# Sparse attention's rotated logits as products over 32 rows in four strips of rows, heads grouped by parity

## What is computed

```python
def block(args):                       # 128 queries at a time
    qf, qi, wi, qc = args
    s_idx = jax.nn.relu(jnp.einsum('bqhd,bkd->bqhk', qi, k_idx))
    score = jnp.einsum('bqh,bqhk->bqk', wi, s_idx)
    score = jnp.where(adm[None], score, -jnp.inf)
    _, sel = lax.top_k(score, topk)    # 128 keys a query
    ...
    logits = jnp.einsum('bqhc,bqkc->bqhk', qf, kv_sel) * scale
    p = jax.nn.softmax(logits, axis=-1)
    return jnp.einsum('bqhk,bqkc->bqhc', p, kv_sel[..., ROPE_DIM:])
```

## Time and profile before

| | |
|---|---|
| median of 3 runs | 2895.94 us (2895.63 to 2901.64) |
| span of the profiled execution | 2884.6 us |
| PE busy in the span | 2535.0 us (88%) |
| DVE busy in the span | 1498.1 us (52%) |
| chain that ended last: PE / DVE / DMA | 60% / 18% / 13% |
| sparse stage, in the span | about 376 to 628 us |
| L952 and L953, records | 80 and 80 |
| L1138 on POOL | 32 operations, median 602 ns |

### The profile page before, as it was taken

The page is one execution under the profiler, slowest core; times in us unless marked ns, Lnnn a source line. Parts: engine busy times, 40 slices in busy tenths (PEclk is TensorE's granted clock), DMA queues, the critical chain, the costliest instruction groups (busy, mean ns, idle before and its releaser), DMA issues.

```text
span 2884.6 us, 35666 instructions
## 1 busy us (share of the span) xinstructions
PE 2535.0 (88%) x14451; PEld 1940.8 (67%) x14451; DVE 1498.1 (52%) x3249; ACT 841.2 (29%) x1455; POOL 793.1 (27%) x755
## 2 busy tenths in 40 slices
PE   5997898889687878769989976789999999999998
PEld 5684544357444444448766566689999989998887
DVE  3125655645200000014543999869987878764443
ACT  2114322233100000014432237734333333333332
POOL 0002310000100000010000139745565656633342
PEclk8997999999799999988999988799999999999999
DMA  8224400014599999963114003799999999989995
GB/s 319 116 88 179 175 30 29 30 61 175 214 422 420 423 421 423 421 266 111 63 54 182 30 26 112 242 375 351 362 388 378 376 354 375 387 334 357 346 357 198
DMA packets 192104, 719.00 MB, mean 249 GB/s; under 512 B 32248, under 2 KB 69152, under 8 KB 162752
## 3 DMA queue, kind: packets, MB, share of 16 engines
q1 hardware_dynamic: 128960, 490.15, 43.7%
q0 software_dynamic: 62976, 226.52, 20.5%
HBM read 659.06 MB, written 57.16 MB: 248 GB/s over the span
## 4 chain that ended last, share of the span: by engine, by line
PE 60%; DVE 18%; DMA 13%; ACT 3%; issue 3%; POOL 2%; SPq 1%; POOLq 0%; DVEq 0%; ACTq 0%
PE psum L3286 9%; PE psum L3273 9%; DMA arena<-w 8%; PE psum L1592 5%; PE psum L426 4%; PE psum L2648 4%; PE psum L2112 4%; PE psum L3235 3%; PE psum L929 3%; DVE arena L3422 3%; DVE rounded L3371 3%; PE psum L1599 2%; DMA arena<-v_rows,arena 2%; PE psum L1201 2%; PE psum L1216 1%
## 5 line engine op out<-in xcount | busy, mean ns | idle before, releaser
L3286 PEld LDWEIGHTS psum<-rounded,rounded 128*128 128x128 f32 x3072 | 453.1, 189 | 34.6 <-issue 30.0
L3286 PE MATMUL psum<-rounded,rounded 128*128 128x320 f32 x3072 | 463.9, 311 | 10.6 <-ACT arena L3338 8.0
L3273 PEld LDWEIGHTS psum<-rounded,rounded 128*128 128x128 f32 x2880 | 426.0, 189 | 28.4 <-issue 13.9
L3273 PE MATMUL psum<-rounded,rounded 128*128 128x320 f32 x2880 | 434.8, 311 | 7.9 <-DVE rounded L3371 4.5
L3222 POOL DMA_INDIRECT arena<-u_rows,arena x192 | 279.6, 1456 | 254.9 <-DVE arena L3422 150.3
L1592 PE MATMUL psum<-arena 128*64 128x256 f32 x2048 | 261.7, 420 | 82.2 <-issue 61.6
L3312 ACT ACTIVATE rounded<-arena 128x1024 fp32r<-128x1024 f32 x248 | 256.9, 1050 | 263.0 <-PE psum L3286 187.1
L3371 DVE TENSOR_TENSOR rounded<-arena,rounded 128x1024 fp32r<-128x1024 f32 x248 | 303.1, 1222 | 18.4 <-ACT rounded L3312 18.4
L1592 PEld LDWEIGHTS psum<-arena 128*64 128x64 f32 x2048 | 183.8, 152 | 172.2 <-issue 123.7
L3222 POOL DMA_INDIRECT arena<-v_rows,arena x192 | 217.4, 1132 | 237.2 <-PE psum L3235 158.2
L1704 DVE COPY arena<-psum 128x256 f32<-128x256 f32 x32 | 13.6, 425 | 445.5 <-PE psum L1645 445.5
(11 more groups left out here) (453 smaller groups left out, 3337.4 us busy)
## 6 DMA issues: line engine op xcount, KB each, us to landing
arena<-w SPq DMA_DIRECT2D x96, 2048.0 KB, 25.8
arena<-v SPq DMA_DIRECT2D x64, 1024.0 KB
arena<-uT SPq DMA_DIRECT2D x60, 1024.0 KB
arena<-wada SPq DMA_DIRECT2D x12, 2048.0 KB
arena<-wp SPq DMA_DIRECT2D x10, 2048.0 KB
arena<-gd SPq DMA_DIRECT2D x60, 320.0 KB
gd<-arena SPq DMA_DIRECT2D x8, 2048.0 KB, 16.3
xb<-arena SPq DMA_DIRECT2D x1, 12032.0 KB, 42.1
```

The source lines that it names most:

```text
L3273: ins = pe.matmul(PS[:, b, 0:DT], w[:, x, k, :], hv[:, y, :], k == 0 and i == 0, k == 7 and i == 2)
L3286: ins = pe.matmul(PS[:, b, 0:DT], w[:, y, x, :], gg[:, z, :], x == 0 and i == 0, x == 7 and i == 2)
```

## The change

The rotated products are done over 32 rows instead of 128. A strip of 32 rows of the array holds the 16 rows of two heads, 2h and 2h + 1, so `QM` now leaves one head of the two: it is masked by the parity of the head, and a group g is the heads of one parity (0, 2, 4, 6 and 1, 3, 5, 7) instead of the first or last four. The four products of a group lie in four different strips of rows (`tile_position`). In blocks 0 to 2 each head of the group gets a bank of its own, 0 to 3. In block 3 two heads are done at a time, since each needs two banks.

The order on TensorE is changed with it: first the latent products of all heads of a batch (four heads, two in block 3), then all their rotated products, where before each head had its own two products in a row. `QM` is made once a block, for both groups, in two buffers; GpSimd first adds three pairs of mask columns into `PARITY`. `OLAT` and `QLAT` are indexed by head 2h + g.

```diff
+    def logit_bank(n, h):
+        return h if n < 3 else 2 * (h % 2)
...
-            pe.wait_ge(*D.po["qm", n, g])
-            for h in range(4):
-                b = 2 * (h % 2)
-                claim(*range(b, b + np_))
+            pe.wait_ge(*D.po["qm", n])
+            for hs in ((0, 1, 2, 3),) if np_ == 1 else ((0, 1), (2, 3)):
+                for h in hs:
+                    b = logit_bank(n, h)
+                    claim(*range(b, b + np_))
+                    for i in range(np_):
+                        pe.matmul(PS[:, b + i, 0:w], QLAT[:, 2 * h + g, 128 * n:128 * n + 128], CKT[:, i * w:i * w + w],
+                                  True, False)
                 for i in range(np_):
-                    pe.matmul(PS[:, b + i, 0:w], QLAT[:, 4 * g + h, 128 * n:128 * n + 128], CKT[:, i * w:i * w + w], True, False)
-                    ins = pe.matmul(PS[:, b + i, 0:w], QM[:, h, :], KR[:, i * w:i * w + w], False, True)
-                ins.then_inc(*D.pe("logits", n, g, h))
+                    for h in hs:
+                        r0 = 32 * h
+                        ins = pe.matmul(PS[:, logit_bank(n, h) + i, 0:w], QM[n % 2][r0:r0 + 32, g, :],
+                                        KR[r0:r0 + 32, i * w:i * w + w], False, True, tile_position=(r0, 0))
+                        if i == np_ - 1:
+                            ins.then_inc(*D.pe("logits", n, g, h))
...
     def sparse_po(po):
-        before = None
+        m8 = CST[:, C_M8:C_M8 + 8]
+        po.tensor_tensor(PARITY, m8[:, 0:2], m8[:, 2:4], ALU.add).then_inc(*D.po("parity", 0))
+        for x in (1, 2):
+            po.wait_ge(*D.po["parity", x - 1])
+            po.tensor_tensor(PARITY, PARITY, m8[:, 2 + 2 * x:4 + 2 * x], ALU.add).then_inc(*D.po("parity", x))
+        po.wait_ge(*D.po["parity", 2])
         for n in range(4):
+            if n > 1:
+                po.wait_ge(*D.pe["logits", n - 2, 1, 3])
             for g in range(2):
-                if before is not None:
-                    po.wait_ge(*before)
-                for h in range(4):
-                    ins = po.tensor_scalar(QM[:, h, :], RB[:, 128 * n:128 * n + 128],
-                                           CST[:, C_M8 + 4 * g + h:C_M8 + 4 * g + h + 1], None, ALU.mult)
-                ins.then_inc(*D.po("qm", n, g))
-                before = D.pe["logits", n, g, 3]
+                ins = po.tensor_scalar(QM[n % 2][:, g, :], RB[:, 128 * n:128 * n + 128], PARITY[:, g:g + 1], None, ALU.mult)
+            ins.then_inc(*D.po("qm", n))
```

More of the change, by code:

```diff
@@ L883, in build @@
     RS = [at(o_va + TK * i, TK) for i in range(2)]
-    QM = at3(o_va + 2 * TK, 4, 128)
+    QM = [at3(o_va + 2 * TK + 256 * i, 2, 128) for i in range(2)]
     PB = at3(OW, 4, TK)
@@ L892, in build @@
     SM = at(o + 12, 4)
-    assert o + 16 <= ARENA
+    PARITY = at(o + 16, 2)
+    assert o + 18 <= ARENA
     GAB = at3(2 * RING, 16, T)
@@ L946, in logits @@
             nk, np_, w = keys_of(n)
-            pe.wait_ge(*D.po["qm", n, g])
-            for h in range(4):
-                b = 2 * (h % 2)
-                claim(*range(b, b + np_))
-                for i in range(np_):
-                    pe.matmul(PS[:, b + i, 0:w], QLAT[:, 4 * g + h, 128 * n:128 * n + 128], CKT[:, i * w:i * w + w], True, False)
-                    ins = pe.matmul(PS[:, b + i, 0:w], QM[:, h, :], KR[:, i * w:i * w + w], False, True)
-                ins.then_inc(*D.pe("logits", n, g, h))
-                for x in range(b, b + np_):
-                    bank[x] = D.dv["logits", n, g, h]
+            pe.wait_ge(*D.po["qm", n])
[6 more added lines that the diff above has]
+                                  True, False)
+                for i in range(np_):
+                    for h in hs:
[4 more added lines that the diff above has]
+                            ins.then_inc(*D.pe("logits", n, g, h))
+                for h in hs:
+                    b = logit_bank(n, h)
+                    for x in range(b, b + np_):
+                        bank[x] = D.dv["logits", n, g, h]
         def latent(n, g):
@@ L1037, in sparse_ac @@
                 ac.wait_ge(*D.pe["latent", n, g])
-                ac.activation(OLAT[:, 4 * g:4 * g + 4, 128 * n:128 * n + 128], PS[:, 6, :].rearrange("p (a b) -> p a b", a=4),
-                              ACT.Copy).then_inc(*D.ac("latent", n, g))
+                ac.activation(OLAT[:, :, 128 * n:128 * n + 128].rearrange("p (h g) t -> p g h t", g=2)[:, g],
+                              PS[:, 6, :].rearrange("p (a b) -> p a b", a=4), ACT.Copy).then_inc(*D.ac("latent", n, g))
                 before = D.pe["latent", n, g]
```

## The result

| | before | changed | |
|---|---|---|---|
| median of 20 runs | 2898.86 us | 2910.42 us | ratio 1.0044, 95% interval 1.0028 to 1.0061 |
| lowest and highest | 2883.52, 2906.57 | 2896.09, 2926.13 | |
| span of the profiled execution | 2884.6 us | 2912.6 us | +28.0 |
| sparse stage in it | 251.1 us | 262.7 us | +11.6 |
| end of the stage to end of span | 2256.0 us | 2272.3 us | +16.3 |

The change makes the kernel 12.8 us slower by the ratio (8 to 18), where 8.6 was forecast (2904.5, range 2899 to 2910).

A forecast was written before the change was run, and what follows sets the result against it. VectorE's start and duration were taken to bound blocks 1 and 2, TensorE block 3. Terms 0.9 + 0.8 + 1.6 + 1.3 + 1.6 + 1.6 + 0.8 = 8.6 us gave span 2893.2, plus 11.3: 2904.5 us, range 2899 to 2910.

The forecast's parts named there:

- Which engine bounds: Sparse stage: VectorE's start and duration count in blocks 1 and 2, (0, 0) alike; TensorE bounds block 3.
- The first add at 5c + 0.4: Blocks 0 to 2, c one full product's time: VectorE's first add 1.6, 2.7, 3.8 us after the group's first product.
- Four strips at once: Rotated products on TensorE: four strips run together, so a set costs c, the time of one full product.
- The two changes of shape: TensorE, between full rows and strips: 0.2 us each way.
- VectorE's pace: Add and maximum per head: about 0.57 us at 144 columns, 0.91 at 272, 1.13 at 400.
- the groups with a slow clock: Groups (0, 1) and (1, 1), logits made at half clock: +0.8 and +1.3 us.
- two more stretches of 3.4 us: High end of the forecast's spread: two more stretches at half clock, within a loss of 13.3 us.
- signs of being wrong: Rotated product starting before the last latent ends, first add by 5c/2 or sooner, or slow clock without a pause ahead.
- The base: Time the loss was added to: profiled span 2884.6 us and 11.3 us around it.
- TensorE as the bound after all: Rival, blocks 0 to 3: TensorE's shorter part counts, -7.8 us, 2888.1 us; chance 0.06.
- Strips that don't overlap: Rival: strips overlap in pairs or not at all, each set c or 3c more, 2907 to 2916 us; chance 0.10.
- The clock that gives it back: Rival: slow stretches fall into longer pauses, loss 4.8 us, 2900.7 us, no change; chance 0.22.

The follow-up runs named there:

- e4: Kernel before plus unneeded TensorE products in its pauses, three per group of block 1, six per group of block 2: stage 242.8 us, ratio 0.9959 to before.
- e3: Changed kernel plus unneeded TensorE products in its pauses, four per group of block 1, six per group of block 2: stage 257.1 us, ratio 0.9996 to before.
- e2: Changed kernel with the rotated products in strips first, then each head's latent products: stage 251.4 us, ratio 1.0008 to before.
- g1: Changed kernel plus one unneeded TensorE product per group of blocks 1 and 2, in the pauses: stage 266.4 us, ratio 1.0049 to before, one run of each.
- f3: Changed kernel with four gates moved into TensorE's pauses of blocks 1 and 2: stage 234.0 us, ratio 0.9944 to before.
- e1: Kernel before with only the changed order and banks, products over full rows, no strips: stage 263.1 us, ratio 1.0026 to before.
- g2: Changed kernel plus unneeded TensorE products in pauses, two per group of block 1, three per group of block 2: stage 259.0 us, ratio 1.0060, one run of each.
- f2: Changed kernel with strips first, then each head's latent products, and four gates moved into TensorE's pauses of blocks 1 and 2: stage 221.0 us, ratio 0.9917 to before.

## Why the prediction was right and wrong

**Which engine bounds** was right, and with it the sign: the kernel got slower, by more than the noise. In (1, 0) the chain runs through VectorE, and TensorE's wait for the copy grew from 2.9 us to 4.1:

```profile
PE psum L986 <- DVE arena L1137: 4.1, 1, 4.1
...
PE psum L979 <- DVE arena L1130: 0.9, 1, 0.9
```

I had named 5.4. The second line is where most of the rest went: the gate now ends before the last division (L1130), so TensorE waits there too, 6.9 us in the stage, which I had not seen coming. It costs nothing by itself, since VectorE is the later one.

**The first add at 5c + 0.4** was right to 0.01 us at 272 columns, and to 0.05 in the others: 1.62 us at 144 columns (1.6), 3.75 at 400 (3.8) and 3.07 in block 3 (3.1). Four strips at once was right too. The two changes of shape, put at 0.2 us each, took 0.3 together at 144 and 272 columns and 0.4 at 400. The chain of block 3, answering:

```profile
591.16 1.78 PE psum L958 x8
592.95 1.14 PE psum L963 x8
594.09 0.70 DVE arena L1121
...
596.18 1.16 PE psum L958 x4
597.33 1.09 PE psum L963 x8
598.42 7.08 PE psum L934 x16
```

The chain goes over to VectorE between the two batches, as I had it: TensorE waits for the banks. The gate starts 7.35 us after the group's first product (598.35 - 591.00; 7.12 before, 7.5 forecast).

**VectorE's pace** was misread. The adds of the kernel before stand 0.91 us apart, and that is 2c = 0.92, the pace of TensorE's two products a head, not VectorE's own. With the logits ready VectorE needs 0.82 us a head, and 1.09 at 400 columns. So having all heads at once did win something: (1, 0) cost 1.3 us and not 1.6, (2, 0) 1.4. The adds of block 2 in the kernel before, 1.34 us apart, are at 2c as well.

**The term that failed is "the groups with a slow clock"**: +0.8 for (0, 1) and +1.3 for (1, 1), and nothing for TensorE's work behind VectorE's copy. Block 0 held (+1.9 for 1.7). Block 1 was forecast at 1.6 + 1.3 = 2.9 and measured 7.8. What follows the copy in (1, 1), before and in the changed kernel:

```profile
493.90 2.18 PE L972 MATMUL psum<-arena 128*128 128x512 f32 x4 [2.70 <-DVE arena L1123]
496.01 8.83 PE L929 MATMUL psum<-arena 128*128 128x512 f32 x16
...
500.94 4.07 PE L986 MATMUL psum<-arena 128*128 128x512 f32 x4 [4.08 <-DVE arena L1137]
504.94 9.60 PE L934 MATMUL psum<-arena 128*128 128x512 f32 x16
```

Up to this point block 1 lost 1.3 us in (1, 0) and 2.1 in (1, 1), 3.4 us, near the 2.9 of the forecast. The other 4.4 us lie behind the copy, where I had put nothing: the second piece of `latent` went from 2.2 to 4.0 us in (1, 0) and from 2.1 to 4.0 in (1, 1), and the gate from 8.8 to 9.5, all by half clock. I let the stretch of 3.4 us stay as it was and only asked whether it would fall into the pause. It became 10.2 us, twice, and in (1, 0) to (1, 1) took in the products L986, all the logits and the head of the gate. TensorE had taken up work again at 477.18 and did not pause, yet the clock stayed at half until 486.00. I had a bound of two more stretches of 3.4 us in the range; the four stretches of blocks 1 and 2 grew by 20.4 us together, six such stretches and not two, 13.6 us of it in block 1. In block 2 it went the other way (1.4 for 3.2): its longer stretches lay in the pauses, and the kernel before had paid for half clock there as well, 5.0 us by e4. The Trainium skill says that pauses of TensorE between bursts throw the clock back (TensorE: Matmul & The Clock Gate, "HAM oscillation"). The trace agrees in the kernel before, where the slow stretches of blocks 1 and 2 go when the pauses are filled, with 8.4 us; in e3 it agrees only in part, since the stretch at 513.4 follows no long pause. That is one of the signs of being wrong that I had named, a slow stretch with no pause ahead of it.

**The base** added its part: 2895.94 us of three runs became 2898.86 of twenty. The measured 2910.42 lies 0.4 us outside the range; with the difference alone, 11.6 us of medians, it would have lain inside. The 5.9 us between forecast and measurement are 2.9 of base, 4.9 too little in block 1, 1.8 too much in block 2, and 0.1 too much elsewhere.

**The rivals.** TensorE as the bound after all: no, its logits got shorter and the stage longer. Strips that don't overlap: no, a set lies in 0.74 us. The clock that gives it back: the other way round. The Trainium skill's warning on reading PSUM (TensorEngine Tiling (Array Packing), "PSUM Bottleneck") names the right engine, but the loss is not that VectorE is slower than TensorE; it is when its first input comes, as e2 shows, which keeps both and loses nothing that the runs can tell.

What stays open: why half clock lasts 3.4 us in one case and 10.2 in another, why 6.8 us stand at 513.4 in e3 behind no long pause, and why a 6.8 us stretch stands at 438 us in e3, g1 and f3 and not in the changed kernel's own profile. Of the kernels in the changed order, the three without it (the changed one, e1, g2) have their first slow stretch 2.6 us behind the stage's start, the three with it 2.9 us. If the changed kernel itself has it in some of its runs, that would give a stage of 266 us in those; the wider spread of its runs (30 us against 23) would fit. It was not shown.

## What to carry to other kernels

When several products are batched to run side by side, look at when the consumer gets its **first** input, not at how much the producer saves; put the batched part first and let each piece finish by itself, and the same strips cost nothing that these runs can tell. Where TensorE waits for VectorE, shortening TensorE's work only makes pauses, and these pauses can cost more than they seem by the clock that falls behind them. Fill them with other products that are needed anyway: here that was worth 27 us of stage (18 by the ratio), and the strips in the right order 1 to 3 us.

## What the runs showed of the hardware

- Four strips of 32 rows run at once: the whole set of four 32-bit products spans 0.74 us at 272 columns, where a single full-row product spans 0.62.
- Products over 32 rows and one over 16 rows share the array. In f2 the two records of a 16-row product start at 471.47 and 472.00 (the first is the last of the x3 in the lines above), and six of the set's eight records start at 471.48 beside them, though the 16-row product stands ahead of the whole set in the program. The other two start at 472.43. I take these for the strip that the 16-row product occupies; the records don't name the strip. There is no change of shape to pay between the two: 0.01 us lies between their starts.
- VectorE's add and maximum of 272 columns take 0.82 us a head when the logits lie ready, and 1.09 at 400. In the kernel before they stood 0.92 and 1.34 us apart, the time of TensorE's two products a head; the records of the operations are as long in both (0.44 at 272).
